# A PSUM bank order of eight for the second weight pair, and VectorE constants and a weight split in another order

## What is computed

```python
def _even_proj(xn, w_in, b_gate):
    q_a, k_a, v_a, o_a, i_a, f_a, q_b, k_b, v_b = _split(xn @ w_in, EVEN_SPLITS)
    log_i = i_a.astype(f32) + b_gate[:H_A].astype(f32)
    log_f = jax.nn.log_sigmoid(f_a.astype(f32) + b_gate[H_A:].astype(f32))
...
def step(carry, inp):                       # one chunk of 128 tokens of mLSTM
    b = jnp.cumsum(fc, axis=-1)
    d_log = jnp.where(causal, b[..., :, None] - b[..., None, :] + ic[..., None, :], -jnp.inf)
    m_t = jnp.maximum(b + m[..., None], jnp.max(d_log, axis=-1))
    s = jnp.einsum('bhtk,bhsk->bhts', qc, kc) * jnp.exp(d_log - m_t[..., None])
...
```

## Time and profile before

| | us |
|---|---|
| three runs | 1647.46, 1640.14, 1648.87 |
| median | 1647.46 |
| the profiled execution, device time | 1647.23 |
| its span from the first to the last instruction | 1645.6 |
| TensorE busy with matmuls | 1576.3 (96%) |
| VectorE busy | 882.5 (54%) |
| ScalarE busy | 597.9 (36%) |
| mean granted TensorE clock over the span | 0.982 |

### The profile page before, as it was taken

The page is one execution under the profiler, slowest core; times in us unless marked ns, Lnnn a source line. Parts: engine busy times, 40 slices in busy tenths (PEclk is TensorE's granted clock), DMA queues, the critical chain, the costliest instruction groups (busy, mean ns, idle before and its releaser), DMA issues.

```text
span 1645.6 us, 31526 instructions
## 1 busy us (share of the span) xinstructions
PE 1576.3 (96%) x12414; PEld 1421.7 (86%) x12414; DVE 882.5 (54%) x1578; ACT 597.9 (36%) x959; POOL 94.3 (6%) x173
## 2 busy tenths in 40 slices
PE   7899998999989999999999999999899999999996
PEld 6799986344459999999999989988799999999995
DVE  5555554456544743544443756877565444544445
ACT  5222224444625432222232634355454331222333
POOL 0000002234220000000000000000000000000000
PEclk9999999999989999999999999999999999999998
DMA  5312218799762222322222311223321322222211
GB/s 183 107 71 97 71 47 315 282 349 335 281 262 78 77 77 77 102 76 76 102 76 77 112 55 54 102 82 126 115 101 54 103 76 76 102 76 76 102 52 56
DMA packets 50603, 195.14 MB, mean 119 GB/s; under 512 B 7406, under 2 KB 9615, under 8 KB 36691
## 3 DMA queue, kind: packets, MB, share of 16 engines
q1 hardware_dynamic: 35938, 139.49, 24.4%
q0 software_dynamic: 14576, 54.41, 8.8%
HBM read 182.19 MB, written 11.68 MB: 118 GB/s over the span
## 4 chain that ended last, share of the span: by engine, by line
PE 81%; DVE 9%; ACT 3%; DMA 3%; issue 1%; SPq 1%; POOLq 0%; POOL 0%; DVEq 0%; ACTq 0%
PE ps L311 23%; PE ps L313 22%; PE ps L312 22%; DMA kbuf<-in_k_cache_dram 3%; DVE wlo L300 2%; PE ps L1355 2%; PE ps L1382 1%; SPq L1334 1%; ACT whi L296 1%; PE ps L1590 1%; DVE s0b L2368 1%; PE ps L1548 1%; PE ps L1494 1%; PE ps L416 1%; PE ps L417 0%
## 5 line engine op out<-in xcount | busy, mean ns | idle before, releaser
L311 PE MATMUL ps<-xhi,whi 128*128 128x280 f32 x2112 | 627.6, 297 | 28.2 <-DVE wlo L520 11.2
L313 PE MATMUL ps<-xhi,wlo 128*128 128x280 f32 x2112 | 620.3, 294 | 0.0
L312 PE MATMUL ps<-xlo,whi 128*128 128x280 f32 x2112 | 619.4, 293 | 0.0
L311 PEld LDWEIGHTS ps<-xhi,whi 128*128 128x128 f32 x2112 | 402.5, 191 | 37.3 <-issue 22.3
L312 PEld LDWEIGHTS ps<-xlo,whi 128*128 128x128 f32 x2112 | 401.6, 190 | 0.4
L313 PEld LDWEIGHTS ps<-xhi,wlo 128*128 128x128 f32 x2112 | 401.8, 190 | 0.0
L300 DVE TENSOR_TENSOR wlo<-raw,whi 128x2048 fp32r<-128x2048 f32 x97 | 222.3, 2291 | 195.9 <-ACT whi L296 195.2
L296 ACT ACTIVATE whi<-raw 128x2048 fp32r<-128x2048 f32 x96 | 183.5, 1911 | 384.8 <-PE ps L313 384.8
L311 PE MATMUL ps<-dhi,whi 128*128 128x280 f32 x1024 | 300.9, 294 | 5.0 <-DVE wlo L300 4.6
L313 PE MATMUL ps<-dhi,wlo 128*128 128x280 f32 x1024 | 300.6, 294 | 0.0
L312 PE MATMUL ps<-dlo,whi 128*128 128x280 f32 x1024 | 299.7, 293 | 0.0
(11 more groups left out here) (412 smaller groups left out, 1431.6 us busy)
## 6 DMA issues: line engine op xcount, KB each, us to landing
raw<-in_weights_dram SPq DMA_DIRECT2D x98, 1024.0 KB, 4.9
kbuf<-in_k_cache_dram SPq DMA_DIRECT2D x128, 256.0 KB, 5.3
vbuf<-in_v_cache_dram POOLq DMA_DIRECT2D x128, 256.0 KB, 8.6
s0b<-in_gla_in_dram POOLq DMA_DIRECT2D x4, 1024.0 KB, 5.2
out_dram<-s0b POOLq DMA_DIRECT2D x4, 1024.0 KB, 4.1
hT<-in_x_dram SPq DMA_DIRECT2D x2, 1120.0 KB, 9.4
out_dram<-pj POOLq DMA_DIRECT2D x2, 1120.0 KB, 8.8
hT<-in_x_dram POOLq DMA_DIRECT2D x2, 1120.0 KB, 13.6
```

Source lines behind the costliest of these rows:

```text
L311: pe.matmul(out, whi[:, par, t, :], hi, start=first, stop=False)
L312: pe.matmul(out, whi[:, par, t, :], lo, start=False, stop=False)
L313: return pe.matmul(out, wlo[:, par, t, :], hi, start=False, stop=last)
```

## The change

Four things are different.

1. Pair 1 has its own TensorE function, `pair_turned_pe`. Output n goes to bank (n + 2) modulo 8. Outputs 0 to 5 go to banks 2 to 7, output 6 to bank 0 and output 7 to bank 1. The waits for `p_rs` (bank 0 read by ScalarE) and `gate_ev` (bank 1 read by VectorE) stood ahead of the whole pair and now stand ahead of outputs 6 and 7. `pair_dve` gets `turn=2` to read the same banks.
2. `cols_dve` is cut in two. The constants, and the copy to `mst`, form `state_dve`, which runs ahead of VectorE's part of pair 1. Only the two copies to `gts` are left in `cols_dve`.
3. The low part of pair 2's second slab, which ended VectorE's part of pair 1, now stands behind `cols_dve`.
4. The waits on `ev` that follow from the banks are new: 15 and 16 for outputs 0 and 1 of pair 2, 11 for `rows_pe` (bank 4), 14 for the first head's `L1065` (banks 4 to 7).

```diff
--- before.py
+++ after.py
@@ -367,8 +367,28 @@
                         pe.wait_ge(S["lo"], i * 2 + (SLAB0[name] + par + 3))
                     for f in range(2):
                         n = 4 * h + 2 * par + f
-                        pe.wait_ge(S["ev"], EV[name] + (n + 1 if i == 1 and n < 4 else i * 8 + n - 3))
+                        if name == "even" and i == 2 and n < 2:
+                            pe.wait_ge(S["ev"], EV[name] + n + 15)
+                        else:
+                            pe.wait_ge(S["ev"], EV[name] + (n + 1 if i == 1 and n < 4 else i * 8 + n - 3))
                         output_pe(pe, n % 4, par, f, h)
+                        beside(n)
+
+        def pair_turned_pe(pe, beside):
+
+            for h in range(2):
+                for par in range(2):
+                    if h == 0:
+                        pe.wait_ge(S["lo"], SLAB0["even"] + par + 5)
+                    for f in range(2):
+                        n = 4 * h + 2 * par + f
+                        if n < 6:
+                            pe.wait_ge(S["ev"], EV["even"] + n + 3)
+                        elif n == 6:
+                            pe.wait_ge(S["p_rs"], 2)
+                        else:
+                            pe.wait_ge(S["gate_ev"], 4)
+                        output_pe(pe, (n + 2) % 8, par, f, h)
                         beside(n)
 
         def pair_pe(pe, i, name, beside=None):
@@ -383,7 +403,7 @@
                         if beside:
                             beside(n)
 
-        def pair_dve(dve, i, name, r, beside=None, split1=True, banks=8, gain=(None,) * 4, behind=None, src=None, split0=5):
+        def pair_dve(dve, i, name, r, beside=None, split1=True, banks=8, gain=(None,) * 4, behind=None, src=None, split0=5, turn=0):
 
             for n in range(8):
                 if beside:
@@ -393,9 +413,9 @@
                 dve.wait_ge(S["done"], i * 8 + (DONE[name] + n + 1))
                 out = pj[:, bass.ds(i * 4 + n % 4, 1), COLS[n // 4]].rearrange("p a n -> p (a n)")
                 if gain[n % 4] is None:
-                    dve.tensor_tensor(out, ps[:, n % banks, 0:HALF], r[:, n // 4], ALU.mult).then_inc(S["ev"], 1)
+                    dve.tensor_tensor(out, ps[:, (n + turn) % banks, 0:HALF], r[:, n // 4], ALU.mult).then_inc(S["ev"], 1)
                 else:
-                    dve.scalar_tensor_tensor(out, ps[:, n % banks, 0:HALF], gain[n % 4], r[:, n // 4], ALU.mult, ALU.mult)\
+                    dve.scalar_tensor_tensor(out, ps[:, (n + turn) % banks, 0:HALF], gain[n % 4], r[:, n // 4], ALU.mult, ALU.mult)\
                        .then_inc(S["ev"], 1)
                 if behind:
                     behind(n)
@@ -537,14 +557,12 @@
                 if n == 7:
                     pe.wait_ge(S["ev"], 2)
                     gates_pe(pe)
-                    pe.wait_ge(S["p_rs"], 2)
-                    pe.wait_ge(S["gate_ev"], 4)
             first_pair_pe(pe, "even", normed_k(pe, "even"), beside)
 
             def rows(n):
                 if n == 7:
                     rows_pe(pe)
-            pair4_pe(pe, 1, "even", rows)
+            pair_turned_pe(pe, rows)
             for i in range(2, PAIRS["even"]):
                 pair4_pe(pe, i, "even", lambda n: mlstm_pe(pe, i, n) if i - 2 < H_A else ahead_pe(pe, n))
 
@@ -573,8 +591,10 @@
             pair_dve(dve, 0, "even", r_first, factor_dve(dve, "even"), gain=(None, float(P) ** -0.5, None, None))
             gates_dve(dve)
             rows_dve(dve)
-            pair_dve(dve, 1, "even", r_first, banks=4, gain=(None, float(P) ** -0.5, None, None))
+            state_dve(dve)
+            pair_dve(dve, 1, "even", r_first, turn=2, gain=(None, float(P) ** -0.5, None, None), split1=False)
             cols_dve(dve)
+            split_lo(dve, SLAB0["even"] // 2 + 2, 1)
             for i in range(2, PAIRS["even"]):
                 pair_dve(dve, i, "even", r_first, banks=4, gain=(None, float(P) ** -0.5 if i < H_A else None, None, None),
                          behind=lambda n: mlstm_dve(dve, i, n) if i - 2 < H_A else ahead_dve(dve, n),
@@ -1017,25 +1037,25 @@
             own.link(dve.tensor_tensor(R(R_WK), R(R_WK), R(R_A), ALU.add))
             dve.tensor_copy(R(R_T), R(R_M)).then_inc(S["rows2"], 1)
 
-        def cols_dve(dve):
+        def state_dve(dve):
+
             own.link(dve.tensor_tensor(four[:, :], ident[:, 0:32], ident[:, 32:64], ALU.add))
             own.link(dve.tensor_tensor(four[:, :], four[:, :], ident[:, 64:96], ALU.add))
             own.link(dve.tensor_tensor(four[:, :], four[:, :], ident[:, 96:128], ALU.add))
-
             own.link(dve.memset(gts[:, :, :], 1.0))
-            dve.wait_ge(S["gt"], 1)
-            dve.tensor_copy(gts[:, 0:4, :], ps[:, 4, 0:64].rearrange("p (c q) -> p c q", q=16))
-            own.link(dve.tensor_copy(gts[0:T4, 4, :], ps[0:T4, 4, 64:80]))
             own.link(dve.memset(hx[:, :, :], 1.0))
             own.link(dve.memset(vx[:, :, P:P + 1], 1.0))
             own.link(dve.memset(qm[:, :], 0.0))
-
             own.link(dve.tensor_copy(mst[:, :], rows[:, R_M, SAMP0 + DEC_T - 1:META0:DEC_T]))
-            dve.sem_inc(S["gts_ok"], 1)
+
+        def cols_dve(dve):
+            dve.wait_ge(S["gt"], 1)
+            dve.tensor_copy(gts[:, 0:4, :], ps[:, 4, 0:64].rearrange("p (c q) -> p c q", q=16))
+            dve.tensor_copy(gts[0:T4, 4, :], ps[0:T4, 4, 64:80]).then_inc(S["gts_ok"], 1)
 
         def rows_pe(pe):
 
-            pe.wait_ge(S["ev"], EV["even"] + 8)
+            pe.wait_ge(S["ev"], EV["even"] + 11)
             pe.wait_ge(S["r_e"], 3)
             for c in range(5):
                 n = P if c < 4 else T4
@@ -1061,7 +1081,7 @@
                 else:
                     pe.wait_ge(S["m_st"], h)
                     pe.wait_ge(S["m_mix"], h)
-                pe.wait_ge(S["ev"], EV["even"] + 8 * h + 8)
+                pe.wait_ge(S["ev"], EV["even"] + (8 * h + 8 if h else 14))
                 pe.matmul(ps[:, 7, :], sel, rows[:, R_RM, 0:SEQ], start=True, stop=True)
                 pe.matmul(ps[0:T4, 6, 0:T4], sel[:, 0:T4], rows[:, R_RM, SEQ:N_TOK], start=True, stop=True)
                 pe.matmul(ps[:, 6, 64:68], sel, rows[:, R_W, P - 1:SEQ:P], start=True, stop=True)
```

## The result

| | before | after |
|---|---|---|
| median of nine runs | 1644.91 us | 1633.73 us |
| lowest and highest | 1640.14, 1648.87 | 1630.90, 1642.27 |
| the profiled execution | 1647.23 us | 1633.73 us |
| its span | 1645.6 us | 1632.1 us |
| its mean granted clock | 0.982 | 0.984 |

The ratio is 0.9941, with a 95% interval of 0.9924 to 0.9959: 9.7 us faster, between 6.7 and 12.5. The median, 1633.7 us, lies in the range of the prediction, 1630 to 1642. Of all executions in this document one, of the kernel under "The gates' wait put back", took 1938.13 us at a mean granted clock of 0.748; it is in no ratio, mean or median here.

The account below looks back on a forecast made before the run. TensorE was busy for 96% of the span, so only its idle time and lost clock could come back. Terms 2.25 + 2.30 + 1.6 + 2.55 + 3.15 = 11.85 us off 1647.23 gave 1635.4, predicted as 1635.5, range 1630 to 1642.

Parts of the forecast that it names:

- (a): Behind the gates, ahead of pair 1: TensorE goes straight on instead of waiting for the gates' taking out, 2.25 us gained.
- (b): Ahead of output 4 of pair 1: it has its own bank and needs only pair 0 out, 2.30 us gained.
- (c): Outputs 4 to 7 of pair 1: no half clock behind the gap ahead of output 4, 1.6 us gained.
- (d): Ahead of the first head's L1065: no wait for the tail of `cols_dve`, 2.55 us gained, 2.0 us to spare at the tightest.
- (e): From the first head's L1065 to the second's: no half clock behind that gap, 3.15 us gained.
- (f): Low part of pair 2's second slab, now behind `cols_dve`: ready before TensorE wants it, costs nothing.
- Only the idle time comes back: Rival for the three gaps: 7.1 us gained, clock losses depend on the one execution; 1640 us, chance 17%.
- The gap behind the gates stays: Rival ahead of pair 1: the gap is TensorE's own start into new code, 2.25 us not gained; 1637.8 us, chance 6%.
- TensorE waits somewhere else instead: Rival ahead of pair 2: VectorE is late and TensorE waits as long as in three places before; 1647 us, chance 4%.
- The clock falls because of the eight banks: Rival in pair 1: each output at half clock costs 3.12 us more, all eight give 1660.5 us; chance 2%.

Follow-up runs that it names:

- The gates' wait put back: The changed kernel with the waits for gates out and sums out again ahead of all of pair 1: 0.9959, 3.5 us over the changed kernel.
- VectorE's half alone: The kernel before with constants ahead of pair 1 and the low part behind `cols_dve`, four banks and waits as before: 0.9990, median 1642.46 us.
- TensorE's half alone: The changed kernel with VectorE's order of before, keeping the eight turned banks and later gate waits: 0.9966 of the kernel before, median 1639.06 us.
- the kernel with four memsets: The changed kernel with the memset of hx done four times, 2.4 us more on VectorE ahead of pair 1: 0.9942 of the kernel before.
- the filled kernel before: The kernel before with 16, 16 and 18 extra matmuls, results never used, in its three gaps: 1.0000 and 0.9988, mean 1644.3 us over 24 runs.
- the 29 runs of the kernel before: The unchanged kernel, run beside the first repeat of the changed kernel, its two halves and the first kernel with filled gaps: median 1644.96 us.
- the 24 runs: The unchanged kernel, run beside the second repeat, the four memsets, the second run with filled gaps and the changed kernel with extra matmuls: median 1644.95 us.
- the 23 runs: The unchanged kernel, run beside the kernels with gates' wait, constants or low part put back and the one with nine memsets: median 1645.59 us.

## Why the prediction was right

**(a) The wait behind the gates, 2.25 us.** Gone. Put back, it came back with 2.25 us of idle and cost 3.5 us (3.8 in the trace), as the clock fell behind it. That the clock stayed at 2.4 GHz behind this gap was true of one execution only. But this does not make the term too low for the change as a whole. In the kernel before, output 4 had to wait for VectorE, which came to output 0 at 60.96 whatever TensorE's clock was. What TensorE loses ahead of that, it waits less there: in the trace of VectorE's half alone it lost clock behind the gates, came to output 4 at 60.72 in place of 59.16, and the wait was 3.07 us and not the 4.6 expected. So in the kernel before a loss of this size behind the gates is hidden by the wait of 2.30 us.

**(b), (c) The wait ahead of output 4, 2.30 us, and the clock behind it, 1.6.** Both gone: no wait, and one clock of 1.00 from 44.4 to 69.2. VectorE's half alone shows what this wait becomes without the banks, 3.07 us. In the two traces that have this gap (2.30 and 3.07 us) the clock fell behind it each time, for 3.4 to 3.5 us; where it was filled, it did not. No run undid (b) alone.

**(d), (e) The wait ahead of the first L1065, 2.55 us, and the clock, 3.15.** Both gone, 37.34 us from head to head. TensorE's half alone brings them back: 2.57 us of wait, half clock for 6.8 us, and 5.5 us in all against 5.7; over many executions 0.9966 against 0.9938, 4.6 us. The spare time at the tightest place was 2.0 in the prediction, 2.2 to 2.3 in the trace and by the kernel with four memsets. The other times were right to 0.5 us: L1085 at 73.33 for 73.8, the second head at 110.74 for 111.2.

**(f) The second slab's low part, nothing.** Right; it costs nothing in either place (0.9938, 0.9940). What I had not said in the prediction is that one of VectorE's two edits would have been enough.

**The size.** The terms to the second head summed to 11.85, and the three traces of the changed kernel show 12.1 against the one of the kernel before. Over many executions the whole kernel gained 10.4 us, uncertain by about 1.5; by the ratio of the nine runs 9.7, between 6.7 and 12.5. The sum is at or just beyond the edge of this. If it is too high, the clock, (c) and (e), is the part that rests on one execution, but this is not shown: in each trace with the second or the third gap the clock fell behind it, about as long as before. The executions with a trace were not typical ones either, 1.8 us over the mean of the kernel before, and on average 2.1 under that of the changed kernel. Where the rest goes in other executions stays open.

The forecast's 1635.5 is 1.8 us over the median of 1633.7. It took 1647.46, the median of three, as the kernel's time, and nine runs gave 1644.9. That start was 2.5 us too high, and the gain between the medians, 11.2, was 0.8 under the forecast's 12.0. The two errors partly cancel, and that is luck.

**The rivals.** "Only the idle time comes back", 7.1 us: the mean gain of 10.4 is 3.3 above it, more than its uncertainty, so it is not the whole. It was right that the clock behind a gap can differ between executions, as behind the gates it did. "The gap behind the gates stays": refuted, both ways. "TensorE waits somewhere else instead": refuted, there is no wait from 38 to 130 us. "The clock falls because of the eight banks": refuted, the granted clock was 1.00 throughout and TensorE had no wait between the outputs of pair 1. The Trainium skill ("TensorE: Matmul & The Clock Gate", section "A second HAM failure mode: psum-queue depth-cycling") tells of a kernel that cycled through its PSUM banks and in which TensorE idled briefly between groups of matmuls, so often that its clock went up and down. The groups of this kernel follow each other without such a pause, so its traces say nothing against that observation; the prediction stretched it when it priced a loss from the bank order alone.

## What to carry to other kernels

Look at what an engine waits for in each gap, and follow the new order in time on all engines that wait for each other before you count a gap as gone: here the two halves of the change brought 5.6 and 1.6 us alone and 10 together. Where a bank order puts a slow consumer's buffers first, turning the order cost nothing here and gave each of its waits the length of some outputs to hide behind. A clock loss read from one profile is one draw: compare the granted clock over several executions before you put a figure on it. And ask what comes next on the path: clock that is lost ahead of a wait for another engine is hidden by that wait, and counts only once the wait is gone. When a kernel with extra work is slower than its own time explains, follow the traces to their end; here 4.3 us lay far behind the place of the edit.

## What the runs showed of the hardware

The granted clock fell behind the gap of 2.25 us in two of three executions and stayed up in one, with the same instructions ahead of it. Behind gaps of 2.30, 3.07, 2.55 and 2.57 us it fell in every trace that has them, for 3.4 us (the first two) and 6.8 us (the last two). It also fell with no gap of more than 0.3 us ahead, at 82.8 and 83.7 us in the two traces of the filled kernel before, where in the traces with no waits at all the same small matmuls left it at 1.00.

Executions of one kernel spread over some 10 us, and their time goes with their mean granted clock. Over the 29 runs of the kernel before the correlation is -0.75, with 1.3 us for each 0.001 of clock; over the 24 runs it is -0.60, with 1.1 us. Of the 23 runs one does not fit, 1650.50 us at 0.936; the other 22 have -0.86 and 1.4 us.

In two of three traces of kernels with extra matmuls TensorE paused 2.5 to 2.6 us at one place of unchanged code near 1056 us, 1.0 us or less in all other traces. The cause is not known.
